# Turning x1 by a product with a diagonal of 1/rms, where it was normed on DVE and transposed: a two-layer diffusion trunk on one core

## The reference, cut to what matters

```python
def rms_norm(x, g):
    y = xf * lax.rsqrt(jnp.mean(xf * xf, axis=-1, keepdims=True) + NORM_EPS)
    return (y * g.astype(jnp.float32)).astype(x.dtype)
...
x = x + gt_m * rms_norm(y, norm_g[i, 1])
hf = modulate(rms_norm(x, norm_g[i, 2]), sh_f, sc_f)       # h * (1 + scale) + shift
x = x + gt_f * rms_norm(sqrelu_mlp(hf, ffn_w1[i], ffn_w2[i]), norm_g[i, 3])
```

## Time and profile before

| | us |
|---|---|
| three timed runs | 938.7, 937.57, 938.67 |
| median of these | 938.67 |
| the profiled execution, device time | 937.01 |
| its span in the trace | 935.1 |
| PE busy | 914.9 |
| DVE busy | 649.3 |
| ACT busy | 431.1 |

### The profile page before, as it was taken

The page is one execution under the profiler, slowest core; times in us unless marked ns, Lnnn a source line. Parts: engine busy times, 40 slices in busy tenths (PEclk is TensorE's granted clock), DMA queues, the critical chain, the costliest instruction groups (busy, mean ns, idle before and its releaser), DMA issues.

```text
span 935.1 us, 11415 instructions
## 1 busy us (share of the span) xinstructions
PE 914.9 (98%) x4623; PEld 753.6 (81%) x4623; DVE 649.3 (69%) x622; ACT 431.1 (46%) x523; POOL 53.2 (6%) x83
## 2 busy tenths in 40 slices
PE   8889999999999999999999999999999999999996
PEld 6658888888888888889888888898888888888885
DVE  6786397589678866696766545757857864783688
ACT  6654484454346333354222224555634624543463
POOL 3002110010001001000101000000000000000001
PEclk9999999999999999999999999999999999999999
DMA  9999889527735576324656531273871661275124
GB/s 306 349 350 359 210 220 327 183 74 215 256 114 139 187 288 226 112 90 158 209 179 217 194 113 46 84 276 123 238 270 34 169 214 57 72 204 174 45 46 179
DMA packets 91403, 170.86 MB, mean 183 GB/s; under 512 B 4270, under 2 KB 34066, under 8 KB 91352
## 3 DMA queue, kind: packets, MB, share of 16 engines
q1 hardware_dynamic: 83912, 155.25, 48.5%
q0 software_dynamic: 7440, 14.89, 8.1%
HBM read 163.81 MB, written 6.32 MB: 182 GB/s over the span
## 4 chain that ended last, share of the span: by engine, by line
PE 52%; DVE 1%; issue 1%; ACT 0%; DVEq 0%
PE ps L674 17%; PE ps L676 17%; PE ps L675 17%; PE ps L768 1%; DVE y L1580 0%; DVE in_lo L1591 0%; PE ps L703 0%; DVE y L1945 0%; DVE xs L1956 0%; ACT in_hi L1209 0%; DVE y L1586 0%; DVE y L1474 0%; DVEq L137 0%; DVE y L1543 0%; DVE st L1949 0%
## 5 line engine op out<-in xcount | busy, mean ns | idle before, releaser
L674 PE MATMUL ps<-in_hi,w_parts 128*128 128x512 f32 (+1 forms) x784 | 290.1, 370 | 0.9 <-DVE in_lo L1591 0.5
L675 PE MATMUL ps<-in_lo,w_parts 128*128 128x512 f32 (+1 forms) x784 | 288.1, 367 | 0.0
L676 PE MATMUL ps<-in_hi,w_parts 128*128 128x512 f32 (+1 forms) x784 | 288.1, 367 | 0.0
L1422 DVE TENSOR_TENSOR w_parts<-raw,w_parts 128x2048 fp32r<-128x2048 f32 x81 | 185.5, 2290 | 125.5 <-ACT w_parts L1102 125.4
L1102 ACT ACTIVATE w_parts<-raw 128x2048 fp32r<-128x2048 f32 x81 | 154.8, 1911 | 214.4 <-PE ps L676 194.4
L674 PEld LDWEIGHTS ps<-in_hi,w_parts 128*128 128x128 f32 x784 | 147.8, 188 | 29.4 <-issue 3.3
L676 PEld LDWEIGHTS ps<-in_hi,w_parts 128*128 128x128 f32 x784 | 147.8, 188 | 24.5
L675 PEld LDWEIGHTS ps<-in_lo,w_parts 128*128 128x128 f32 x784 | 147.8, 189 | 24.1
L674 PE MATMUL ps<-w_parts,ops_hi 128*128 128x512 f32 x280 | 109.1, 389 | 0.2 <-DVE y L1474 0.2
L675 PE MATMUL ps<-w_parts,ops_hi 128*128 128x512 f32 x280 | 109.0, 389 | 0.0
L676 PE MATMUL ps<-w_parts,ops_lo 128*128 128x512 f32 x224 | 87.2, 389 | 0.0
(11 more groups left out here) (203 smaller groups left out, 1040.2 us busy)
## 6 DMA issues: line engine op xcount, KB each, us to landing
raw<-in_ffn_w_dram SPq DMA_DIRECT2D x57, 1024.0 KB, 5.5
ada_raw<-in_ada_w_dram SPq DMA_DIRECT2D x56, 512.0 KB, 6.2
xs<-in_ffn_w_dram SPq DMA_DIRECT2D x14, 1024.0 KB, 5.4
xs<-in_ffn_w_dram POOLq DMA_DIRECT2D x10, 1024.0 KB, 8.7
raw<-in_conv_in_w_dram SPq DMA_DIRECT2D x16, 512.0 KB, 5.3
raw<-in_ada_w_dram SPq DMA_DIRECT2D x4, 1024.0 KB, 11.1
ada_sum<-in_ada_w_dram SPq DMA_DIRECT2D x4, 1024.0 KB, 12.2
win<-in_ada_w_dram SPq DMA_DIRECT2D x4, 1024.0 KB, 11.9
```

What stands on the lines that cost most here:

```text
L674: nc.tensor.matmul(o, hi, b_hi, start=start, stop=False, skip_group_check=on)
L675: nc.tensor.matmul(o, hi, b_lo, start=False, stop=False, skip_group_check=on)
L676: return nc.tensor.matmul(o, lo, b_hi, start=False, stop=stop, skip_group_check=on)
L1422: nc.vector.tensor_tensor(w_lo[:, u % W_SLOTS, :], raw_of(u), w_hi[:, u % W_SLOTS, :].bitcast(F32), ALU.subtract).then_inc(w_lo_ready, 1)
```

## The change

`first_norm` becomes `first_diag`. DVE no longer writes the normed row of 1024; it multiplies the 128x128 identity with the tile's column of 1/rms and writes this diagonal into the first 128 columns of `y_tok[:, t, :]`. `turn_first` no longer transposes the normed rows: it is a plain float32 product with a square of `xs` as the weights and the diagonal as the moving side. For square X (tokens by features) and diagonal D that is the transpose of X times D, so each token's column comes out scaled by its own 1/rms. The number of instructions that the program names on each engine, and their order, stay as they were.

Since the turns now read `xs` itself, the store and the overwriting of `xs` behind it may not run ahead of them: `save_x` of layer 0 waits for all eight groups (`x1_turned`) where it waited for the four norms (`x1_norm`).

```diff
             def save_x(layer):
                 if layer == 0:
-                    sp.wait_ge(x1_norm, NT)
+                    sp.wait_ge(x1_turned, len(FIRST_TURNED))
                     sp.wait_ge(x1_sq, NT)
...
             def turn_first(side, pair):
-                pe.wait_ge(x1_norm, 2 * side + 2)
+                pe.wait_ge(x1_diag, 2 * side + 2)
...
-                        tr = nc.tensor.transpose(o[:, n, toks(t)], y_tok[:, 2 * side + t, (2 * pair + n) * P:(2 * pair + n + 1) * P], ident[:, :])
+                        tr = nc.tensor.matmul(o[:, n, toks(t)], xs[:, 2 * side + t, (2 * pair + n) * P:(2 * pair + n + 1) * P], y_tok[:, 2 * side + t, 0:P], start=True, stop=True)
                 tr.then_inc(x1_turned, 1)
...
-            def first_norm(t):
+            def first_diag(t):
                 dve.wait_ge(x1_rms, t + 1)
                 nc.vector.reciprocal(st0[:, 7, t:t + 1], st0[:, 6, t:t + 1]).then_inc(x1_rcp, 1)
                 dve.wait_ge(x1_rcp, t + 1)
-                nc.vector.tensor_scalar(y_tok[:, t, :], xs[:, t, :], st0[:, 7, t:t + 1], None, ALU.mult).then_inc(x1_norm, 1)
+                nc.vector.tensor_scalar(y_tok[:, t, 0:P], ident[:, :], st0[:, 7, t:t + 1], None, ALU.mult).then_inc(x1_diag, 1)
```

More of the change, by code:

```diff
@@ L248, in trunk @@
         y0_sq, y0_copied, y0_gated, y0_sum, y0_rms, y0_rcp = sem("y0_sq"), sem("y0_copied"), sem("y0_gated"), sem("y0_sum"), sem("y0_rms"), sem("y0_rcp")
-        x1_new, x1_sq, x1_rms, x1_rcp, x1_norm = sem("x1_new"), sem("x1_sq"), sem("x1_rms"), sem("x1_rcp"), sem("x1_norm")
+        x1_new, x1_sq, x1_rms, x1_rcp, x1_diag = sem("x1_new"), sem("x1_sq"), sem("x1_rms"), sem("x1_rcp"), sem("x1_diag")
         x1_turned, xt_copied, f_made, f_hi, f_lo = sem("x1_turned"), sem("xt_copied"), sem("f_made"), sem("f_hi"), sem("f_lo")
@@ L1887, in _ @@
             first_x(2)
-            first_norm(0)
-            first_norm(1)
+            first_diag(0)
+            first_diag(1)
             columns(8)
@@ L1893, in _ @@
             first_x(3)
-            first_norm(2)
-            first_norm(3)
+            first_diag(2)
+            first_diag(3)
             first_input(1)
```

## The result

The changed kernel is slower by 0.45%: 942.15 us (median of 9 runs) against 938.35 us (median of 9 runs of the kernel before on the same chip), a ratio of 1.0045 with a 95% interval of 1.0031 to 1.0059. A second set on another chip gave 941.67 against 938.79 us, 1.0029 (1.0018 to 1.0041). The forecast was 942.0.

The account below looks back on a forecast made before the run. PE was taken to bound the kernel, with next to no idle time behind the first turn. Products +3.9, earlier first turn -0.5 and store 0 gave +3.4 us, on the median of 938.67 a forecast of 942.0 us, range 939.7 to 944.3.

Parts of the forecast that it names:

- PE's part: In the turns, 32 plain products replace 32 transpositions, two records against one: 8.08 - 4.21 = 3.9 us loss.
- DVE's part: Ahead of the first turn, a shorter diagonal replaces the norm, so the turn starts earlier: 0.5 us gain.
- The store: On SP, the store waits for the last turn and goes out 8.4 us later, covered, so it costs nothing.
- Nothing given back later: Behind the turns no load-paced stretch returns PE's added time; the rival, 940 and below, shared 0.15 with another.
- hidden second pass: Rival in the turns: a product's second record costs PE almost nothing; 938.2 us, chance 0.15 together with time returned later.
- four slots: Rival in the turns: each product holds PE for four transpositions' time, 12.5 us less 0.5; 950.7 us, chance 0.02.
- late store: Rival behind the turns: the store lands very late, unit 8 is late and PE stands; 947.8 us, chance 0.04.
- The marks: Sign in the new profile: the same 3.4 us shift at every later mark of PE behind the last turn.

Follow-up runs that it names:

- changed, fewer records: The changed kernel without the nine products of ones with the identity in its first 10 us; 942.18 us, ratio 1.0046 to the kernel before.
- products alone: The kernel before with only its 32 transpositions made plain float32 products with the identity; 942.45 against 938.79 us, ratio 1.0037.
- each product twice: The changed kernel with each of the 32 products issued twice into the same place; 949.16 us, ratio 1.0111 to the kernel before.

## Why the prediction was right, point by point

- **PE's part (3.9 us).** Right in kind and nearly in size. The eight groups in the undisturbed trace (changed, fewer records) hold PE 1.07, 1.08, 1.99 (two), 0.98, 0.90, 0.99 and 0.92 us, together 7.93, where I took 8.08 from L927. Less 4.21 that is 3.7 us, and products alone show 3.73 from A to B (3.53 against the second trace of the kernel before).
- **DVE's part (-0.5 us).** Right. The diagonal takes 0.28 us for the 0.25 taken; the first turn starts 3.31 us after A where it was 3.76 (4.06 in the second trace), a gain of at least 0.45. From A to B, the change without a dip is 23.07, which is 3.21 over before and 0.52 under products alone. Here the gain is kept: the second group of turns is longer by 0.5 us, and `add_up` behind it, which waited 0.36 us for its load with transpositions and an early first turn, shows no wait. That the longer group covers that wait is argued from these rows, not tested.
- **The store (0).** Right in its result. Its working was off in three places. Landing took 7.6 us and not 13.4; fewer loads shared the DMA engines with it (304 GB/s in those 7.6 us with the store's own 2 MB among them, 388 GB/s in the 13.4 before). The loads into `xs` were held by `load(5)` and not by the store, in the kernel before already, as the earlier trace rows show (landed at 87.3, issued at 89.33), so they had more room than the working gave them. And at 24 us of delay what is late first is the load of unit 6; unit 8 comes behind it.
- **Nothing given back later.** Right: 32 products more cost their 7.5 us in full. But I had named only time given back as what could happen behind the turns. A new wait of 0.8 us arose at 161 that no step of the sum has, most likely by way of the instruction load. With it the change is 3.2 + 0.8 = 4.0 us in the traces, and 4.0 in the runs of the second set at a mean granted clock of 0.997 or over; the medians of the two sets gave 3.8 and 2.9.
- **The number.** That 942.0 came so near to 942.15 is partly luck. The sum of 3.4 us is 0.6 under the 4.0 of the undisturbed traces, since it has 0.2 too much for the products and nothing for the new wait; and the median it was added to, of three runs, lay 0.3 us above that of the nine.
- **The rivals.** The hidden second pass and the four slots are out by products alone and by each product twice: two slots. By the Trainium skill, "TensorE: Matmul & The Clock Gate", section "Terms", the transpose mode is four times faster for FP32; the traces do not agree, since 0.97 us against 0.48 for a group is a factor of two. The late store is out at its present place; 24 us further on it costs 10 us, 9 us further on 0.5 to 0.9 us in the trace and more in the medians, which leaves its price there open.
- **The marks.** "Shifts of 3.4 us at each later mark" was 5.7 in the first trace after. The 1.34 us of loads ahead of A and the low clock of 1.1 us from A to B were in it and are not the change's.

## What to carry to other kernels

A turn that also scales is tempting as one product with a diagonal, but in plain float32 it takes two slots of PE where a transposition takes one; it pays only where the other engine's time is on the path, and here PE was full and DVE's gain was the 0.5 us of one wait. Price such an exchange from rows of the same kernel that have the same operation and shape, start to start. And compare single traces from a mark just ahead of the change: more than a third of the difference between the first two traces lay ahead of it or in a clock level that came and went.

## What the runs showed of the hardware that I had not expected

- Where a load of PE's instructions (one packet of queue 8, 0.02 MB) fell 7.3 to 7.9 us after the issue of POOL's add, the add landed after 10.0 to 10.7 us; where it fell 11.5 us after it or later, the add landed after 9.0 to 9.4 us. Its place moves with the number of PE records ahead of it: 64 more moved it by 5 to 6 us. In these traces a change of PE's instruction count so went with 0.8 us of waiting some 80 us away from its place. One trace (each product twice) has the long landing without the load inside it, so this is not the whole cause.
- PE's granted clock fell to 0.5 for about 3.5 us in several traces, of kernels with and without the change: in seven of the thirteen somewhere from 55.9 to 65.4 us, where PE had waited for loads, and in three others between 35 and 40 us. In it the same 12 records of L884 took 2.65 us for 1.60. In the one kernel in which the idle 1.94 us were filled with six products it stayed at 1.00 there; that is one trace, and both of the kernel before, products alone and fewer records kept it there without them.
- The store of 2 MB landed in 7.6 us when it was issued after the rush of loads, in 13.4 us within it.
